# Expert routing and gather of a two-block transformer: tokens kept once in f32, one-hot gather for two experts at a time, sixteen weight places

## The reference

```python
def expert_choice_moe(h, w_router, w_gate, w_up, w_down):
    B, T, D = h.shape
    cap = CAPACITY_FACTOR * T // N_EXPERTS          # 64
    logits = jnp.einsum('btd,de->bte', h, w_router).astype(jnp.float32)
    affinity = jax.nn.softmax(logits, axis=-1)
    gate, idx = lax.top_k(jnp.swapaxes(affinity, 1, 2), cap)
    xe = jax.vmap(lambda hb, ib: hb[ib])(h, idx)
    a = jnp.einsum('becd,edf->becf', xe, w_gate)
    u = jnp.einsum('becd,edf->becf', xe, w_up)
    ye = jnp.einsum('becf,efd->becd', jax.nn.silu(a) * u, w_down) * gate.astype(h.dtype)[..., None]

    def combine(yb, ib):
        return jnp.zeros((T, D), yb.dtype).at[ib.reshape(-1)].add(yb.reshape(-1, D))

    return jax.vmap(combine)(ye, idx)
```

## Time and profile before

| | us |
|---|---|
| median of 3 runs | 2120.62 (2119.46 to 2121.51) |
| profiled execution | 2117.76 |
| its span | 2116.0 |
| PE busy | 1920.8 |
| output projection to first expert product | 679.1 to 715.4 |
| expert products | 715.4 to 1195.1 |

### The profile page before, as it was taken

The page is one execution under the profiler, slowest core; times in us unless marked ns, Lnnn a source line. Parts: engine busy times, 40 slices in busy tenths (PEclk is TensorE's granted clock), DMA queues, the critical chain, the costliest instruction groups (busy, mean ns, idle before and its releaser), DMA issues.

```text
span 2116.0 us, 22864 instructions
## 1 busy us (share of the span) xinstructions
PE 1920.8 (91%) x9497; PEld 1367.7 (65%) x9497; DVE 966.8 (46%) x1580; ACT 628.0 (30%) x1074; POOL 102.8 (5%) x83
## 2 busy tenths in 40 slices
PE   6899998999999699999999678999898889999997
PEld 4777776778876334342332258798686668888886
DVE  4787777742643422221212355322455455434544
ACT  4444444432332100010100033222445433323322
POOL 0110000000000000000000110001221200000000
PEclk8999999999999799999999889999898989999999
DMA  9323332252252399999999721251211313233221
GB/s 312 102 87 103 96 104 90 81 179 99 86 200 80 127 409 409 409 409 409 409 409 409 274 92 55 90 183 40 60 61 59 120 62 105 67 116 105 80 84 40
DMA packets 201114, 355.05 MB, mean 168 GB/s; under 512 B 7122, under 2 KB 148530, under 8 KB 200242
## 3 DMA queue, kind: packets, MB, share of 16 engines
q1 hardware_dynamic: 197264, 338.79, 44.3%
q10 hardware_dynamic: 3458, 14.50, 1.9%
q0 software_dynamic: 288, 0.30, 0.1%
HBM read 345.47 MB, written 8.39 MB: 167 GB/s over the span
## 4 chain that ended last, share of the span: by engine, by line
PE 75%; DVE 10%; DMA 7%; ACT 5%; issue 2%; POOL 2%; SPq 0%; DVEq 0%; ACTq 0%
PE ps L461 73%; DMA rx<-in_w_exp_down 3%; PE ps L464 2%; DMA ring<-in_w_exp_up 2%; POOL tb L2588 2%; DMA rx<-in_w_exp_up 1%; DVE small L2002 1%; DVE wsp1l L1739 1%; ACT M L1138 1%; DVE X L1748 1%; DMA md<-in_w_mod 1%; ACT k2h L1138 1%; ACT tb L1138 1%; DVE onesrow L1748 1%; DVE acc L1748 1%
## 5 line engine op out<-in xcount | busy, mean ns | idle before, releaser
L461 PE MATMUL ps<-H,wsq0h 128*128 128x512 f32 x704 | 222.3, 398 | 17.2 <-POOL H L2588 15.9
L461 PE MATMUL ps<-H,wsp0h 128*128 128x512 f32 x576 | 188.8, 408 | 13.9 <-ACT H L1138 8.0
L461 PE MATMUL ps<-H,wsq1h 128*128 128x512 f32 x544 | 173.6, 401 | 7.0 <-DVE wsq1l L1739 7.0
L461 PEld LDWEIGHTS ps<-H,wsq0h 128*128 128x128 f32 x704 | 134.2, 192 | 47.9 <-issue 20.2
L461 PE MATMUL ps<-rx,XE 128*64 128x512 f32 x656 | 155.8, 600 | 1.6 <-DMA rx<-in_w_exp_up 1.1
L1739 DVE TENSOR_TENSOR wsq0l<-ring,wsq0h 128x1024 fp32r<-128x1024 f32 (+2 forms) x72 | 81.1, 1164 | 131.8 <-ACT wsq0h L1138 131.8
L461 PE MATMUL ps<-H,wsq0l 128*128 128x512 f32 x352 | 139.0, 395 | 0.0
L461 PEld LDWEIGHTS ps<-H,wsp0h 128*128 128x128 f32 x576 | 107.1, 194 | 39.5 <-issue 12.0
L461 PE MATMUL ps<-H,wsp1h 128*128 128x512 f32 x336 | 111.9, 415 | 20.8 <-DVE wsp1l L1739 20.8
L461 PEld LDWEIGHTS ps<-H,wsq1h 128*128 128x128 f32 x544 | 104.6, 194 | 30.3 <-issue 8.6
L1138 ACT ACTIVATE tb<-ps 128x512 f32<-128x512 f32 (+1 forms) x54 | 31.0, 575 | 298.3 <-PE ps L461 298.3
(11 more groups left out here) (339 smaller groups left out, 3587.0 us busy)
## 6 DMA issues: line engine op xcount, KB each, us to landing
rx<-in_w_exp_gate SPq DMA_DIRECT2D x45, 1024.0 KB, 18.2
rx<-in_w_exp_down SPq DMA_DIRECT2D x42, 1024.0 KB, 18.5
ring<-in_w_in SPq DMA_DIRECT2D x39, 1024.0 KB, 5.6
rx<-in_w_exp_up SPq DMA_DIRECT2D x37, 1024.0 KB, 18.5
ring<-in_w_exp_up SPq DMA_DIRECT2D x27, 1024.0 KB, 18.0
ring<-in_w_exp_down SPq DMA_DIRECT2D x22, 1024.0 KB, 18.5
ring<-in_w_up SPq DMA_DIRECT2D x20, 1024.0 KB, 5.2
ring<-in_w_exp_gate SPq DMA_DIRECT2D x19, 1024.0 KB, 18.3
```

What stands on the lines that cost most here:

```text
L461: return pe.e.matmul(o, l, r, start=start, stop=stop, skip_group_check=True)
```

## The change

1. HT holds the turned tokens once, in f32. After the norm ACT multiplies it in place by r4, so R, rth, rtl and DVE's subtraction in `turn_x` go.
2. Logits with tokens on partitions: x1's block is the stationary operand, the router's 16 columns move (4 products for each c). The transposes of the logits go. The bias row is made ahead of `wo`. The squares are summed on PE in two groups of four products in place of DVE's last addition.
3. Slots: the marks are transposed right after the 8 rounds, compared on 128 partitions, and the prefix sum is made by products with a triangle of ones (new constant `tri`) and rows of ones.
4. Gather of two experts at a time: G is f32 with 128 columns, a chunk is 4 f32 products, ACT alone writes XE (scale gA2, bias sh2). In every pair but the last, the gather for the next pair lies in the second expert. `gates` reuses G.
5. G and XE have two buffers of half the size; hs, Y and GT one. The room goes to weights: 16 places (rx6, rx4, rx5, rx0 to rx3, the ring's four, rx7 to rx11). rx0 and rx1 open after the attention projection `pa` (`past_kr`), rx7 to rx11 after `wo`.

```diff
-    HT = at("HT", 8192, F32R, sq)
-    rx = [at(f"rx{i}", 2048, F32, sq + 8192 + 2048 * i) for i in range(5)]
-    rtl = at("rtl", 512, F32R, sq + 18432)
+    HT = at("HT", 4096, F32, sq)
+    rx = [at(f"rx{i}", 2048, F32, sq + 4096 + 2048 * i) for i in range(7)]
+    gr = at("gr", 512, F32, sq + 18432)
...
-    XE = at("XE", 4096, F32, sq + 19648)
-    G = at("G", 2048, F32R, sq + 23744)
-    hs = at("hs", 1024, F32, sq + 25792)
-    hT = at("hT", 1024, F32, sq + 26816)
-    Y = at("Y", 2048, F32, sq + 27840)
-    gr = at("gr", 512, F32, sq + 29888)
-    GT = at("GT", 1024, F32, sq + 30400)
-    rth = at("rth", 512, F32R, sq + 31424)
-    rx += [at(f"rx{5 + i}", 2048, F32, sq + 31936 + 2048 * i) for i in range(2)]
+    selt = at("selt", 64, F32, sq + 19328)
+    XE = at("XE", 2048, F32, sq + 19648)
+    G = at("G", 1024, F32, sq + 21696)
+    hs = at("hs", 512, F32, sq + 22720)
+    hT = at("hT", 1024, F32, sq + 23232)
+    Y = at("Y", 1024, F32, sq + 24256)
+    GT = at("GT", 512, F32, sq + 25280)
...
-    places = [(4, past_v), (2, past_a), (3, past_a), (0, past_m), (1, past_m)]
+    past_kr = [("pe_group", (("pa", 3), 1))]
+    places = [(6, past_v), (4, past_a), (5, past_a), (0, past_kr), (1, past_kr), (2, past_m), (3, past_m)]
...
-    turns += [(f"rx{i}", rx[i], past_h) for i in (5, 6)]
+    turns += [(f"rx{i}", rx[i], past_h) for i in range(7, 12)]
...
+        pe.wait_ge(S["v_route"], "dlb")
+        hold(7, [("v_route", "lg"), ("a_norm", ("x1", "root"))])
+        mm(bank(7, 64, 80), onesrow[0:16, 0:P], dlb, True, True).then_inc(*S["pe_route"].tick("bias2"))
...
+        def logits(c):
+
             if c == 0:
-                hold(6, [("v_route", "lgT")])
+                hold(6, [("v_route", "lg0")])
                 pe.wait_ge(S["v_route"], "wrg")
-            i = mm(ps[0:16, 6 * 512:7 * 512], wrgv[:, c, :], Xv[:, c, :], c == 0, c == 7)
+            pe.wait_ge(S["v_take"], ("x1", c))
+            for i in range(4):
+                t = mm(bank(6, i * 16, i * 16 + 16), Xv[:, c, i * P:(i + 1) * P], wrgv[:, c, :], c == 0 and i == 0, c == 7)
             if c == 7:
-                i.then_inc(*S["pe_route"].tick("logits"))
+                t.then_inc(*S["pe_route"].tick("lg"))
+
+        def squares(src, start):
+            for i in range(4):
+                t = mm(bank(7, i, i + 1), src[:, i * P:(i + 1) * P], ones[:, 0:1], start and i == 0, not start)
+            return t
+
+        def behind_x(c):
+            if c:
+                turn_x(c - 1)
+                logits(c - 1)
...
-                behind=lambda m: 2 * n + m and turn_x(2 * n + m - 1))
-        pe.wait_ge(S["v_norm"], ("x1", 7))
-        hold(7, [("a_norm", ("x1", "root"))])
-        for i in range(4):
-            t = mm(bank(7, i, i + 1), tba[:, i * P:(i + 1) * P], ones[:, 0:1], True, True)
-        t.then_inc(*S["pe_norm"].tick("x1"))
+                behind=lambda m: behind_x(2 * n + m))
+        logits(7)
+        pe.wait_ge(S["v_norm"], ("x1", 6))
+        squares(tba, True)
+        pe.wait_ge(S["a_norm"], ("x1", 7))
+        squares(tbv[1], False).then_inc(*S["pe_norm"].tick("x1"))
...
-        pe.wait_ge(S["v_route"], "dlb")
-        hold(5, [("v_route", "lg")])
-        mm(bank(5, 0, 16), onesrow[0:16, 0:P], dlb, True, True).then_inc(*S["pe_route"].tick("bias2"))
-        hold(4, [("v_route", "lg0")])
-        pe.wait_ge(S["v_route"], "lgT")
-        for i in range(4):
-            t = tr(bank(4, i * 16, i * 16 + 16), lgT[:, i * P:(i + 1) * P], ident[0:16, 0:16])
-        t.then_inc(*S["pe_route"].tick("lg"))
...
-        pe.wait_ge(S["v_route"], "slo")
-        hold(6, [("v_route", "slt")])
+        pe.wait_ge(S["v_route"], ("out", 7))
+        hold(4, [("v_route", "sel")])
         for i in range(4):
-            t = tr(bank(6, i * 16, (i + 1) * 16), slo[:, i * P:(i + 1) * P], ident[0:16, 0:16])
+            t = tr(bank(4, i * 16, (i + 1) * 16), wk[0][:, i * P:(i + 1) * P], ident[0:16, 0:16])
+        t.then_inc(*S["pe_route"].tick("left"))
+
+        pe.wait_ge(S["v_route"], "sel")
+        hold(5, [("v_route", "slt")])
+        mm(bank(5, 0, 64), tri, selt[:, :], True, False)
+        for d in (1, 2, 3):
+            t = mm(bank(5, 16 * d, 64), onesrow[:, 0:P], selt[:, 0:64 - 16 * d], False, d == 3)
...
-            Gq = G[:, q % 2 * 1024:q % 2 * 1024 + 1024].rearrange("p (i n) -> p i n", n=256)
-            b = take(("R", q), [("a_gather", ("R", q))])
-            pe.wait_ge(S["v_route"], "rt")
             pe.wait_ge(S["v_gather"], ("G", q))
-            for i in range(4):
-                for part in (rth, rtl):
-                    t = mm(bank(b, 0, 256), part[:, i * P:(i + 1) * P], Gq[:, i, :], i == 0 and part is rth,
-                           i == 3 and part is rtl)
-            t.then_inc(*S["pe_gather"].tick(("R", q)))
+            pe.wait_ge(S["a_route"], "ht")
             for c in range(8):
-                b = take(("xe", q, c), [("v_gather", ("xe", q, c))])
-                pe.wait_ge(S["v_turn"], ("ht", 7))
+                b = take(("xe", q, c), [("a_gather", ("xe", q, c))])
                 for i in range(4):
-                    for part in range(2):
-                        t = mm(bank(b, 0, 256), htv[part][:, i, c * P:(c + 1) * P], Gq[:, i, :], i == 0 and part == 0,
-                               i == 3 and part == 1)
+                    t = mm(bank(b, 0, P), htv[:, i, c * P:(c + 1) * P], Gb[q % 2][:, i, :, :], i == 0, i == 3)
...
-            taken = gather(pr // 2 + 1) if pr % 2 and pr < 7 else iter(())
+            taken = gather(pr + 1) if pr < 7 else iter(())
...
-        ac_.wait_ge(S["v_route"], "r4")
-        ac_.wait_ge(S["pe_group"], (("wo", 3), 1))
-        act(rth[:, :].rearrange("p (i m) -> p i m", m=P), r4b.to_broadcast([P, 4, P]), ACT.Copy).then_inc(
-            *S["a_route"].tick("rth"))
+        ac_.wait_ge(S["a_turn"], ("ht", 7))
+        for i in range(4):
+            t = act(htv[:, i, :], htv[:, i, :], ACT.Copy, scale=r4[:, i:i + 1])
+        t.then_inc(*S["a_route"].tick("ht"))
...
-            ac_.wait_ge(S["pe_gather"], ("R", q))
-            if q:
-                ac_.wait_ge(S["v_gather"], ("xe", q - 1, 7))
-            act(Rs, bank(where.get(("R", q), 0), 0, 256), ACT.Copy).then_inc(*S["a_gather"].tick(("R", q)))
             for c in range(8):
-                ac_.wait_ge(S["v_gather"], ("xe", q, c))
-                o = XEb[q % 2][:, c, :]
-                act(o, o, ACT.Identity, bias=sh2[:, c:c + 1]).then_inc(*S["a_gather"].tick(("xe", q, c)))
+                ac_.wait_ge(S["pe_gather"], ("xe", q, c))
+                ac_.wait_ge(S["v_route"], "slt")
+                ac_.wait_ge(S["pe_group"], (("wo", 3), 1))
+                if q > 1:
+                    ac_.wait_ge(S["pe_expert"], ("u", 2 * q - 3, 3))
+                act(XEb[q % 2][:, c, :], bank(where.get(("xe", q, c), 0), 0, P), ACT.Identity, bias=sh2[:, c:c + 1],
+                    scale=gA2[:, c:c + 1]).then_inc(*S["a_gather"].tick(("xe", q, c)))
...
-            tt(low, x, h.bitcast(F32), ALU.subtract).then_inc(*S["v_turn"].tick(("ht", c)))
...
-        v.wait_ge(S["pe_route"], "logits")
-        v.wait_ge(S["pe_group"], (("wo", 3), 1))
-        cp(lgT, ps[0:16, 6 * 512:7 * 512]).then_inc(*S["v_route"].tick("lgT"))
...
-        chain(cp(wk[0], ps[0:16, 6 * 512:7 * 512]), "wk")
+        v.wait_ge(S["pe_group"], (("wo", 3), 1))
         for r in range(8):
-            chain(v.e.max(m8, wk[r % 2]), ("max", r))
-            chain(v.e.match_replace(wk[(r + 1) % 2], m8, wk[r % 2], -1.0), ("out", r))
-        chain(ts1(sel, wk[0], 0.0, ALU.is_lt), "sel")
-        chain(v.e.tensor_tensor_scan(slo, onesrow[0:16, :], sel, 0.0, ALU.mult, ALU.add), "scan")
-        tt(slo, slo, sel, ALU.mult).then_inc(*S["v_route"].tick("slo"))
-        v.wait_ge(S["a_route"], "rth")
-        tt(rtl[:, :].rearrange("p (i m) -> p i m", m=P), r4b.to_broadcast([P, 4, P]),
-           rth[:, :].bitcast(F32).rearrange("p (i m) -> p i m", m=P), ALU.subtract).then_inc(*S["v_route"].tick("rt"))
+            w = wk[r % 2] if r else ps[0:16, 6 * 512:7 * 512]
+            chain(v.e.max(m8, w), ("max", r))
+            chain(v.e.match_replace(wk[(r + 1) % 2], m8, w, -1.0), ("out", r))
+        v.wait_ge(S["pe_route"], "left")
+        chain(ts1(selt[:, :], bank(4, 0, 64), 0.0, ALU.is_lt), "sel")
         v.wait_ge(S["pe_route"], "slot")
-        chain(cp(slt[:, :], bank(6, 0, 64)), "slt")
+        chain(tt(slt[:, :], bank(5, 0, 64), selt[:, :], ALU.mult), "slt")
...
-        def gather(q):
+        def choose(q):
+
             if q > 1:
-                v.wait_ge(S["pe_gather"], ("done", q - 2))
-            onehot(G[:, q % 2 * 1024:q % 2 * 1024 + 1024].rearrange("p (i e j) -> p i e j", e=4, j=64), 4 * q, 4).then_inc(
-                *S["v_gather"].tick(("G", q)))
-            yield
-            for c in range(8):
-                v.wait_ge(S["pe_gather"], ("xe", q, c))
-                v.wait_ge(S["a_gather"], ("R", q))
-                if q > 1:
```

(53 more changed lines are left out.)

41 lines of the change are left out of this document (18 added, 23 removed).

## The result

The changed kernel takes 2130.3 us (median of 5 runs, 2129.5 to 2135.3), the kernel before 2120.4 (2119.5 to 2121.5): a ratio of 1.0051, 95% interval 1.0036 to 1.0066. It is slower by half a per cent, and 2132 had been forecast. The sum is right; the terms are less so. I go through the trace in the order of time, part by part, and set each stretch beside the same stretch of before.

What follows compares the result with a forecast made beforehand. Before, the expert stage was held bound by DMA (479.7 us) with PE close below (463.4); after, by PE. Terms 15.2 - 6.0 - 1.1 + 0.5 + 3.0 = +11.6 on 2120.6 gave 2132 us, range 2118 to 2139.

Steps and rivals of the forecast that it cites:

- router's weights: Before the output projection: the router's 64 KB load is delayed by slabs issued ahead of it, +3.0 us, bounds 0 and +9.
- output projection: Logits of seven blocks -0.5, bias row ahead of the projection +0.8, larger constants' load +0.2: together +0.5 us.
- routing and chunks ahead: Between output projection and first expert product: shorter routing chain -6.0 us, three gather chunks ahead of the experts -1.1 us.
- stage: Expert stage: 494.9 us instead of 479.7, +15.2, with 1.19 us for each gather chunk.
- The main step: Expert stage: a chunk costs 1.19 us (0.89 + 0.2 + 0.1), so PE exceeds the DMA limit of 466.8: +15.2 us.
- rival of the cheap chunk: Expert stage: switching is hidden, a chunk costs 0.89 us, the stage falls to 476.6; 2114 us in all; chance 0.10.
- weight loads that don't hide: Gather in the expert stage: weight loads show beneath 128 moving columns, 39 us more, 2171 us; chance 0.03.
- The upper end (+9): Router's load: 1040 packets, 65 on each of 16 engines, each behind a slab's 4 KB packet of 0.16 us.
- Rival 2: Before the output projection: the router's load waits in full, +9 us, 2138 us; chance 0.13.
- The likeliest way: Whole kernel: slower, 2132 us, own range 2125 to 2136, with the gather on PE adding 15.2; chance 0.62.
- rival 3: Whole kernel: gain and loss cancel, chunk near 1.0 to 1.05 us, no router delay, 2120 to 2123 us; chance 0.12.
- The signs named: Profile after: chunk to next expert product 1.09, pairs of 63.5 us alike, no slab waits, one-hot 6 us sooner.

Runs made afterwards that it cites:

- Experiment 7: The changed kernel with two gather chunks back to back behind every fourth k step instead of one behind every second: 2122.9 us, ratio 1.0014.
- experiment 5: The changed kernel with only the first of each gather chunk's four products made: 2100.9 us, ratio 0.9912.
- experiment 6: The changed kernel without rx7 to rx11, so eleven places for weights as before: 2130.7 us, ratio 1.0062.
- experiment 3: The kernel before with PE's counter of PSUM banks moved on by 28 behind the expert stage: 2114.1 us, ratio 0.9968.
- experiment 4: The changed kernel with PE's counter of PSUM banks moved back by 28 behind the expert stage: 2134.9 us, ratio 1.0069.
- experiment 1: The changed kernel with rx0 and rx1 again opened only after the merged tensor is split: 2118.8 us, ratio 0.9995.

## Why the prediction was right, and where it was not

In the order of its sum, from the two profiled executions:

| term | forecast | measured | from |
|---|---|---|---|
| up to the router's load | 0 | +0.2 | 618.8, 619.0 |
| router's weights | +3.0 | **+12.2** | 3.8, 16.0 |
| output projection | +0.5 | -0.4 | 56.5, 56.1 |
| routing and chunks ahead | -7.1 | -6.5 | 36.3, 29.8 |
| stage | +15.2 | +12.5 | 479.7, 492.1 |
| behind the stage | 0 | **-5.6** | 920.9, 915.3 |
| sum | +11.6 | +12.4 | 2116.0, 2128.4 |

- **The main step holds.** The stage changes its limit from DMA to PE, because a chunk beside expert products costs 1.19 and not 0.89. Measured: 1.09 + 0.10. Experiment 7 puts the 0.10 at 0.15, see there. Experiments 5, 6 and 7 show the three parts of the step one by one: without most of the gather DMA is the limit again, the five places more give nothing, fewer edges between expert and gather products give back 9.7 us. The rival of the cheap chunk (2114) is out, and that of weight loads that don't hide (2171) too: eight instructions go in 0.99 to 1.09 us.
- **The stage came out 2.7 less than forecast.** 1.15 of it is the first stretch (44.9, not 46.05): PE waited 0.95 us for hs there, and a chunk now lies in that gap; it has no idle time at all (44.90 busy of 44.90). The rest is in the pairs, 63.13 to 63.63 instead of 63.5: two of the eight chunks have expert products on one side only, and cost about 1.0 with everything instead of 1.19, the one behind the turn of hs and the last, behind which the combination comes (823.99 to 824.99).
- **Routing.** -6.5 against -7.1. The logits and transposes that leave the chain gave 6.0 as forecast; the three chunks ahead took 5.24 and not 4.6, since nearly all 24 of their instructions ran at half clock (granted clock 0.50 until 720, 0.22 each) and not 17 of them.
- **The output projection** came out at -0.4 instead of +0.5. The bias row ahead of it cost 0.86, as forecast (+0.8); but a block with its logits takes 6.81 instead of 7.07 us, 0.26 less for each of six and not 0.07.
- **The step that failed** is the price of the router's weights: +3.0 forecast, +12.2 measured. The upper end (+9) counted 65 packets per engine behind one slab packet each, and the Trainium skill's rule was named for it. I took +3 by the time of the constants' load, 6.6 us with 3.5 taken off for an idle DMA. That load was the right case, read the wrong way: by time and not by packets. It is issued at 29.27 while q1 is full, none of its packets moves before 33.25, and then they go one for one. The DMA queues of the kernel before, 34 to 35 us:

```profile
q10 hardware_dynamic: 73, 0.32, 81.0%
q1 hardware_dynamic: 74, 0.08, 21.4%
```

The constants' load has only 144 packets, of some 4 KB, so taking turns cost it little; the router's load has 1040 small ones. With these rows the price could have been worked out: 4 + 1040/98 = 14.6 us instead of 2.25, about +12. Even the upper end was short by 3 us, since it left out the 4 us ahead of the first packet. Rival 2 therefore is what happened in its mechanism (it would have given 2138), and with its price the sum would have been 2141 and off by 11.
- **What was not in the forecast** is the order of the banks, -5.6 in the profile, -6.0 and -4.6 in the medians of experiments 3 and 4. That nothing changes behind the stage stands in no line of the prediction and was not worked out: it was taken from the diff, which has no line there. With the failed step it makes +9.2 - 5.6 - 2.7 - 0.9 + 0.6 + 0.2 = +0.8. The number 2132 is good to 2 us by luck: a term that is 9.2 too low, and an effect of -5.6 that was not thought of together with a stage priced 2.7 too high, have nothing to do with each other and cancel. The likeliest way (slower, by the gather on PE) was right in direction; but experiment 1 shows that with the router's load mended and nothing else the change ends at 2118.8, no slower than before. The loss of the stage is real, and the gains of routing and banks pay for it. That is not rival 3, though the time is near its own (2120 to 2123): its chunk of 1.0 to 1.05 didn't come, and without the banks' 5 us the kernel of experiment 1 would stand near 2124 (an estimate from experiments 3 and 4), slower than before even with the router's load mended.
- **The signs named** came: chunk to next expert product 1.09, pairs alike (63.1 to 63.6 for 63.5), no slab waits, below 409 GB/s, one-hot 6 us sooner behind the projection, the wait for wr longer than 4.2 us.

What stays open: why the first packets of a load take 4 us beside a full stream, and whether the 2.4 us of a fourfold chunk reach the whole time.

## What to carry to other kernels

Before opening a buffer earlier, list the small loads issued just behind that point on any queue: here a load of 1040 small packets that PE waits for paid one large packet of the running stream for each of its own, and 4 us before the first. Price such a load by its packets, and not by the time of another load with other packets. A counter that deals out banks or buffers across stages couples them: an edit in one stage that takes a different number shifts the deal in all later ones, and it can be tested alone, in one line, in either kernel. When two limits lie within 3% of each other, count the edit against both, and count what PE pays to go from one shape of product to another and back: here grouping the small products in twos took 9.7 of the stage's 12.5 us back. And when two kernels are compared with their side effects mended, give both only the mending: an improvement in one of them belongs in a run of its own.

## What the runs showed of the hardware

- A load of 64 KB in packets of 64 bytes takes 2.25 us on an idle DMA and 14.5 us beside a stream of five slabs of 1 MB, on another queue, the first of them issued 1.5 us earlier: 4 us of nothing (1 us on the idle DMA), then its packets and the slabs' one for one, 98 and 97 per us. The load of the constants near 29 us in the kernel before shows the same two: 4.0 us of nothing beside a full q1, then 73 packets of its own to 74. The slabs hardly lose: 97 of their packets per us beside it, 96 without.
- Expert products (64 columns of stationary operand) and gather products (128) cost about 0.35 us for each passage there and back: 0.2 in the gather's products (1.09 for eight, 1.98 for sixteen, 3.77 for 32, 0.89 for each eight more) and 0.15 in the expert products behind (1.87, 3.58, 5.30 for eight, sixteen, 24). In the middle of a run of f32 products with 128 moving columns an instruction takes 0.11 us at a granted clock of 1.00, and 0.22 at half clock.
